# One layer of a sparse-attention, recurrence, cross-attention and product-key-expert block: recurrence gate moved to VectorE, attention units regrouped, cross attention by heads, expert decode in pieces

## The chip, the cores and the metric

One core of one Trainium2 chip (trn2) runs the whole kernel. The metric is the device time of one execution, in microseconds (us).

## The reference

The input `x` is 256 tokens by 1024 features (fp32). In order:

- `h = x @ w_in` gives the queries, keys, values and gates of everything below.
- **Sparse attention** (8 heads of 64, two key groups of four heads): per head a compressed branch (15 blocks of keys), a selected branch (with 4 blocks of 64 and 16 to be chosen, all are chosen, so it is causal attention over 256 keys with `k_slc, v_slc`) and a window branch (window 512, so causal attention with `k_win, v_win`). The branches are summed with sigmoid gates.
- **Recurrence** (4 heads of 128): `f = lb + (1 - lb) * sigmoid(...)`, a gated linear attention with decay `cumsum(log f)`; its output is normalised and multiplied by `norm_w` and by `silu(g)`.
- `x1 = LayerNorm(alpha * x + concat @ w_out)`.
- **Cross attention** over 256 memory tokens, 4 heads of 256: `softmax(q k^T / 16) v @ wo`, then `x2 = LayerNorm(alpha * x1 + ...)`.
- **Product-key experts**: per token and each of 8 heads, the top 16 of 128 + 128 half scores, the top 16 of their 256 sums, an expert number `i1 * 128 + i2` and a softmax gate for each; `a = gelu(down[e] . t) * gate`, `out = sum a * up[e]`, over 16384 experts. Then the last LayerNorm.

## The kernel before, in words

Every large matmul is done in three fp32r terms. A weight tile of 128x1024 fp32 (0.5 MB) is loaded by SyncE's queue into a slot `raw`; ScalarE rounds it to `hi` (`split`, L536); `lo = raw - hi` is made in the place of `raw` by VectorE (`rest`, L694) or by GpSimd (L522) for the tiles from `POOL_FROM` to `POOL_TO`; TensorE multiplies hi*hi, hi*lo and lo*hi (`three`, L1090 to L1092). There are `N1` = 75 stream tiles for all weights but the experts', then 128 `down` tiles and 128 `up` tiles. A tile of kind "T" is 24 matmuls of 256 columns, one of kind "R" 12 matmuls of 512 columns. ScalarE's `split` runs `DEPTH` = 4 tiles ahead. The `raw` ring has `EARLY` = 8 slots for the stream and `RING` = 5 for the experts; SyncE loads tile n once the tile that holds its slot was used. `slot(n)` gives the slot:

```python
return n % EARLY if n < N1 else (n - N1) % RING          # L182
POOL_FROM, POOL_TO = N1 - 4, N1 + 40                     # L179
```

`order()` writes the program order of the first part by hand, and every engine walks the same list in order; engines wait for each other by semaphores. In it the attention units `u` = 0 to 9 and the steps `level(j, t)` of the recurrence stand between weight tiles: per `u` a tile, `level(u-2, 0)`, the transposes of the probabilities of `u` (`turn_probs`), the scores of `u+1`, a tile, `level(u-2, 1)`, the values of `u`. After `level(j, 1)` VectorE merges (L936) and updates the factors `QF`, `KB` and `Fa`/`Fb` (L951 to L953), for which the next `level(j+1, 0)` (L1263) waits. Units 0 to 7 are a branch, a key group `g` and a half `t` of the tokens, four heads each: `scores` (L1140) makes for each head one or two 128-column blocks (L1171) with weights of 64 rows, each diagonal block followed by a matmul that adds the causal mask (L1174).

The gate `silu(g) * norm_w` is made by three GpSimd instructions (L504 to L508) when the `hg` tiles are done. Cross attention is units 10 and 11 (one half of the tokens each, four heads): both follow the eighth `xq` tile, and `turn` 4 and 5 (transposes of `xo`, L1309; rounding L651; rest L977) precede the first `xo` tile. Then come `xo`, the norm, eight `pq` tiles, each followed by `route(h)`: two score matmuls (L1285), and on VectorE the top-16 searches. When all eight are searched, VectorE decodes the positions to expert numbers (L992 to L1015: `picked_e` has 8192 f16 elements a partition), sums the gates (L1017 to L1021) and only then enters the loop over `down` and `up` tiles (`table_order()`), where `softmax` stands at tile 30 and `index` at tile 44. ScalarE writes gelu of each `down` tile (L660).

## Time and profile before

| | |
|---|---|
| median of 3 runs | 1169.48 us (1165.38 to 1171.67) |
| profiled execution, its own time | 1171.79 us |
| its span | 1170.0 us |
| mean granted TensorE clock | 0.971 |
| TensorE matmul / weight load busy | 94% / 85% |
| VectorE busy | 65% |
| ScalarE busy | 44% |
| GpSimd busy | 12% |
| moved from HBM | 183.80 MB, 158 GB/s |

The gelu of the first `down` tile starts at 391.4 us of the span, that of the last at 786.6 us; the `up` tiles take the rest. A group of matmuls that reads "busy" still overlaps its neighbours, so the distance from one start to the next is the time that one costs.

### The profile page before, as it was taken

The page shows a single profiled execution, that of the slowest core. Times are in us where ns is not written, and L with a number is a line of the kernel's source. Part 1 is how long each engine was busy: PE and PEld are TensorE (multiplying, and loading weights), DVE is VectorE, ACT ScalarE, POOL GpSimd, SP SyncE. Part 2 cuts the span into 40 slices and gives each one's busy share as a digit, 9 for nine tenths or more (in the row PEclk, how much of TensorE's full clock was granted, in tenths as well). Part 3 has the DMA queues.
Part 4 walks back from the last instruction along what each step waited for, and adds up shares of the span by engine and source line. Part 5 has one row for each costly group of instructions (what it writes and reads, how often), then busy time and mean ns, then how long its engine had stood idle before and what let it go on. Part 6 is the DMA issues. An engine that isn't in the chain of part 4 may idle for free.

```text
span 1170.0 us, 19066 instructions
## 1 busy us (share of the span) xinstructions
PE 1101.7 (94%) x7790; PEld 996.2 (85%) x7790; DVE 761.5 (65%) x1363; ACT 512.9 (44%) x799; POOL 146.1 (12%) x77
## 2 busy tenths in 40 slices
PE   6999989899869897999999999999999999999995
PEld 6987879779659897999999999998888788888884
DVE  4336555683377999124488888549888886555555
ACT  4244423444333443555544444454444444454451
POOL 3000020000004689930000000000000000000000
PEclk9889979999989999999999999999999999999998
DMA  9642212365031454555555445556555556556551
GB/s 335 220 154 91 80 65 83 114 203 198 28 117 38 163 182 126 179 181 180 180 163 163 163 162 164 179 183 206 172 176 168 178 166 190 186 195 193 188 195 73
DMA packets 50439, 186.62 MB, mean 160 GB/s; under 512 B 5824, under 2 KB 5856, under 8 KB 49840
## 3 DMA queue, kind: packets, MB, share of 16 engines
q1 hardware_dynamic: 48384, 176.71, 45.9%
q0 software_dynamic: 1968, 8.69, 2.2%
q8 instruction: 62, 1.02, 0.4%
q14 instruction: 25, 0.20, 0.1%
HBM read 183.80 MB, written 1.05 MB: 158 GB/s over the span
## 4 chain that ended last, share of the span: by engine, by line
PE 87%; DVE 5%; POOL 3%; ACT 2%; DMA 2%; issue 1%; SPq 0%; DVEq 0%; ACTq 0%
PE psS L1350 15%; PE psG L1090 15%; PE psT L1350 15%; PE psG L1091 14%; PE psG L1092 14%; POOL lo L522 3%; PE psS L1171 2%; PE psO L1334 1%; PE psO L1335 1%; PE psO L1263 1%; DMA raw<-in_down 1%; ACT hi L536 1%; PE psO L1231 1%; DVE lo L694 1%; PE psS L1163 1%
## 5 line engine op out<-in xcount | busy, mean ns | idle before, releaser
L694 DVE TENSOR_TENSOR lo<-raw,hi 128x1024 fp32r<-128x1024 f32 x287 | 350.0, 1221 | 220.2 <-ACT hi L536 219.9
L536 ACT ACTIVATE hi<-raw 128x1024 fp32r<-128x1024 f32 x331 | 350.3, 1059 | 308.1 <-DMA raw<-in_up 191.4
L1090 PE MATMUL psG<-b_hi,hi 128*128 128x256 f32 x1152 | 335.2, 291 | 9.1 <-POOL lo L522 7.5
L1091 PE MATMUL psG<-b_lo,hi 128*128 128x256 f32 x1152 | 329.3, 286 | 0.0
L1092 PE MATMUL psG<-b_hi,lo 128*128 128x256 f32 x1152 | 329.0, 286 | 0.0
L1090 PEld LDWEIGHTS psG<-b_hi,hi 128*128 128x128 f32 x1152 | 224.4, 195 | 11.1 <-POOL lo L522 8.9
L1091 PEld LDWEIGHTS psG<-b_lo,hi 128*128 128x128 f32 x1152 | 224.5, 195 | 0.2
L1092 PEld LDWEIGHTS psG<-b_hi,lo 128*128 128x128 f32 x1152 | 224.3, 195 | 0.0
L522 POOL TENSOR_TENSOR lo<-raw,hi 128x1024 fp32r<-128x1024 f32 x44 | 124.1, 2835 | 124.1 <-ACT hi L536 123.9
L1068 DVE TENSOR_TENSOR act_lo<-H,act_hi 128x256 fp32r<-128x256 f32 x128 | 54.0, 423 | 100.1 <-ACT act_hi L678 100.0
L660 ACT ACTIVATE H<-psG 128x256 f32<-128x256 f32 x128 | 49.1, 383 | 159.7 <-PE psG L1092 159.6
L1350 PE MATMUL psS<-hi,act_hi 128*128 128x512 f32 x256 | 82.3, 402 | 0.0
L1350 PE MATMUL psS<-hi,act_lo 128*128 128x512 f32 x256 | 79.5, 392 | 0.0
L1350 PE MATMUL psT<-hi,act_hi 128*128 128x512 f32 x256 | 79.5, 392 | 0.0
L1350 PE MATMUL psS<-lo,act_hi 128*128 128x512 f32 x256 | 79.4, 391 | 0.0
L1350 PE MATMUL psT<-lo,act_hi 128*128 128x512 f32 x256 | 79.3, 391 | 0.0
L1350 PE MATMUL psT<-hi,act_lo 128*128 128x512 f32 x256 | 79.2, 391 | 0.0
L1090 PE MATMUL psG<-o_hi,hi 128*128 128x256 f32 x192 | 59.2, 308 | 13.7 <-DVE lo L694 10.9
L1091 PE MATMUL psG<-o_lo,hi 128*128 128x256 f32 x192 | 58.0, 302 | 0.0
L1092 PE MATMUL psG<-o_hi,lo 128*128 128x256 f32 x192 | 57.9, 302 | 0.0
L1350 PEld LDWEIGHTS psT<-hi,act_hi 128*128 128x128 f32 x256 | 48.1, 188 | 10.7
L1350 PEld LDWEIGHTS psS<-lo,act_hi 128*128 128x128 f32 x256 | 48.1, 188 | 10.7
(273 smaller groups left out, 1523.3 us busy)
## 6 DMA issues: line engine op xcount, KB each, us to landing
raw<-in_down SPq DMA_DIRECT2D x128, 512.0 KB, 3.7
raw<-in_up SPq DMA_DIRECT2D x128, 512.0 KB, 3.9
raw<-in_w_stream SPq DMA_DIRECT2D x75, 512.0 KB, 3.8
w<-in_w POOLq DMA_DIRECT2D x1, 2048.0 KB, 8.6
xT<-in_xT SPq DMA_DIRECT2D x2, 512.0 KB, 4.7
memT<-in_memT SPq DMA_DIRECT2D x1, 1024.0 KB, 6.7
x_tok<-in_x_tok POOLq DMA_DIRECT2D x1, 1024.0 KB, 5.5
ln_gb<-in_ln_g POOLq DMA_DIRECT2D x2, 512.0 KB, 6.5
```

The lines of the kernel that those rows point to most:

```text
L522: pool.tensor_tensor(lo[slot(n)][:], raw[slot(n)][:], hi[n % DEPTH][:].bitcast(FP32), ALU.subtract)\
L536: act.activation(hi[n % DEPTH][:], raw[slot(n)][:], ACT.Copy).then_inc(hi_done, 1)
L660: act.activation(H[:, j, :], psG[j % 2][:, 0:S], ACT.Gelu).then_inc(h_out, 1)
L694: dve.tensor_tensor(lo[slot(n)][:], raw[slot(n)][:], hi[n % DEPTH][:].bitcast(FP32), ALU.subtract)\
L1068: dve.tensor_tensor(a_lo[j % 4][:], H[:, j, :], a_hi[j % 4][:].bitcast(FP32), ALU.subtract)\
L1090: pe.matmul(out, hi_l, hi_r, start=start, stop=False)
L1091: pe.matmul(out, hi_l, lo_r, start=False, stop=False)
L1092: return pe.matmul(out, lo_l, hi_r, start=False, stop=stop)
L1163: mm = pe.matmul(psS[:, h * S:(h + 1) * S], xq[:, 2 * h + kk, t * P:(t + 1) * P], xk[:, 2 * h + kk, :], start=kk == 0, stop=kk == 1)
L1171: mm = pe.matmul(out, qT[g * HD:(g + 1) * HD, r, t * P:(t + 1) * P], kT[b][g * HD:(g + 1) * HD, kb * P:(kb + 1) * P], start=True, stop=not ...
L1231: mm = pe.matmul(psM[:, kv * G * NC:(kv + 1) * G * NC], w1[:, kv, m, :], blk[:, kv, m, :], start=m == 0, stop=m == CB // 2 - 1)
L1350: mm = pe.matmul((psS, psT)[t][:, c * 512:(c + 1) * 512], left[:, cut], right[:, c * 512:(c + 1) * 512], start=st, stop=sp)
```

## The change

1. **Gate.** The three GpSimd instructions go. VectorE makes the gate in two steps `silu` (one for each half of the tokens, two instructions each), which stand behind the scores of units 7 and 8.
2. **Units.** A unit is now a branch, a pair `g` of head places and a half `t`: two heads of each key group. The mask goes first, one matmul for each of two PSUM banks over 256 or 512 columns, then one matmul for each head over all of its keys, heads of the two groups in turn. The number of exponentials, transposes and values is as before.
3. **Cross attention.** It is done by heads, both halves of the tokens together, in seven stages between the `xq` tiles (two a stage) and the first three `xo` tiles. An `xo` tile waits for its own head's part of `b_lo` alone.
4. **Ring.** The slots of the expert tiles are shifted by `N1 % EARLY` = 3.
5. **GpSimd's tiles** end at `N1 + 24` in place of `N1 + 40`.
6. **Decode.** It is cut into 8 steps at the `down` tiles 22, 24, ... 36, over half of the units of one list each, with layouts whose last dimension is a pair of f16 values; the gate sums follow the last step.

```diff
-UNITS = [(b, g, t) for b in range(2) for g in range(G) for t in range(NT)]
+UNITS = [(b, pair, t) for b in range(2) for pair in range(REP // 2) for t in range(NT)]
...
+        if u in (6, 7):
+            out.append(("silu", u - 6))
...
-    gemm(AT["xo"] - n)
-    out += [("scores", 10), ("turn_probs", 10), ("scores", 11), ("values", 10),
-            ("turn_probs", 11), ("values", 11), ("turn", 4), ("turn", 5)]
+    for stage in range(XH + 3):
+        gemm(2 if stage < XH else 1)
+        out += [(what, stage - lag) for lag, what in ((3, "cross_turn"), (2, "cross_values"), (1, "cross_probs"),
+                                                      (0, "cross_scores")) if 0 <= stage - lag < XH]
...
-POOL_FROM, POOL_TO = N1 - 4, N1 + 40
+POOL_FROM, POOL_TO = N1 - 4, N1 + 24
+DECODE = 8
...
-    return n % EARLY if n < N1 else (n - N1) % RING
+    return n % EARLY if n < N1 else (n - N1 + N1 % EARLY) % RING
...
+        if j >= 22 and j % 2 == 0 and (j - 22) // 2 < DECODE:
+            out.append(("decode", (j - 22) // 2))
...
-            pool.wait_ge(act_took, TAKEN[TILES[AT["hg"]][8] + 1][1])
-            pool.wait_ge(rec_in, 32)
-            pool.tensor_scalar(hg_t[:], hg_t[:], 1.0, 0.5, ALU.add, ALU.mult).then_inc(pool_step, 1)
-            pool.tensor_tensor(hg[:], hg[:], norm_w[:].unsqueeze(1).broadcast_to([P, NT, 512]), ALU.mult)\
-                .then_inc(pool_step, 1)
-            pool.wait_ge(pool_step, 2)
-            pool.tensor_tensor(hg[:], hg[:], hg_t[:], ALU.mult).then_inc(silu_ready, 1)
...
+                elif what == "silu":
+                    dve.wait_ge(act_took, TAKEN[TILES[AT["hg"]][8] + i][1])
+                    step(dve.scalar_tensor_tensor(out=hg[:, i, :], in0=hg_t[:, i, :], scalar=1.0, in1=hg[:, i, :],
+                                                  op0=ALU.add, op1=ALU.mult))
+                    step.wait()
+                    dve.scalar_tensor_tensor(out=hg[:, i, :], in0=hg[:, i, :], scalar=0.5, in1=norm_w[:],
+                                             op0=ALU.mult, op1=ALU.mult).then_inc(silu_ready, 1)
...
+            def decode(i):
+                c, first = i // 4, i // 2 % 2 * PH
+                units = slice(first, first + PH)
+                rows = PH * TOPK // 2
+                e = picked_e[:, c, units].rearrange("p u k a -> p (u k) a")
+                if i % 2 == 0:
+                    step(dve.tensor_tensor(e.rearrange("p n (a b) -> p n a b", b=2),
+                                           iota16[:].unsqueeze(1).broadcast_to([P, rows, TOPK, 2]),
...
+                                           .broadcast_to([P, rows, TOPK, 2]), ALU.is_equal))
+                    step.wait()
+                    step(dve.tensor_tensor(picked_e[:, c, units], picked_e[:, c, units],
...
+                for half in (16, 8, 4):
+                    step.wait()
+                    step(dve.tensor_tensor(e[:, :, 0:half], e[:, :, 0:half], e[:, :, half:2 * half], ALU.add))
...
+                if name == "xo" and i == 0:
+                    pe.wait_ge(cross_lo, k0 // 2 + 1)
...
-                for r in range(REP):
-                    for kb in range(t + 1):
-                        out = psS[:, r * S + kb * P:r * S + (kb + 1) * P]
-                        diagonal = kb == t
-                        mm = pe.matmul(out, qT[g * HD:(g + 1) * HD, r, t * P:(t + 1) * P],
-                                       kT[b][g * HD:(g + 1) * HD, kb * P:(kb + 1) * P], start=True, stop=not diagonal)
-                        if diagonal:
-                            mm = pe.matmul(out, identb[:], causal[:], start=False, stop=True)
+                for group in range(G):
+                    both = psS[:, group * 512:(group + 1) * 512].rearrange("p (j n) -> p j n", n=S)
+                    pe.matmul(both[:, :, 0:keys], identb[:],
+                              causal[:, S - keys:S].unsqueeze(1).broadcast_to([P, 2, keys]), start=True, stop=False)
+                for j in range(2):
+                    for group in range(G):
+                        at = (group * 2 + j) * S
+                        mm = pe.matmul(psS[:, at:at + keys], qT[group * HD:(group + 1) * HD, 2 * g + j, t * P:(t + 1) * P],
+                                       kT[b][group * HD:(group + 1) * HD, 0:keys], start=False, stop=j == 1)
...
+            def cross_scores(h):
+                pe.wait_ge(act_took, TAKEN[TILES[AT["xq"] + 2 * h + 1][8]][1])
+                if h >= 2:
+                    pe.wait_ge(cross_exp, h - 1)
```

On SyncE the loads stand at the change from the `pq` tiles (in_w_stream) to the `down` tiles as follows; `raw_58` to `raw_66` are slots 0 to 4, `raw_107` to `raw_111` slots 5 to 7. Before:

```order
L470 DMA raw_64<-in_w_stream 128x1024 [waits tile_used]
L470 DMA raw_66<-in_w_stream 128x1024 [waits tile_used]
L470 DMA raw_107<-in_w_stream 128x1024 [waits tile_used]
L470 DMA raw_109<-in_w_stream 128x1024 [waits tile_used]
L470 DMA raw_111<-in_w_stream 128x1024 [waits tile_used]
L470 DMA raw_58<-in_w_stream 128x1024 [waits tile_used]
L470 DMA raw_60<-in_w_stream 128x1024 [waits tile_used]
L470 DMA raw_62<-in_w_stream 128x1024 [waits tile_used]
L470 DMA raw_58<-in_down 128x1024 [waits tile_used]
L470 DMA raw_60<-in_down 128x1024 [waits tile_used]
L470 DMA raw_62<-in_down 128x1024 [waits tile_used]
```

Now, from the last three `pq` tiles on:

```order
L482 DMA raw_58<-in_w_stream 128x1024 [waits tile_used]
L482 DMA raw_60<-in_w_stream 128x1024 [waits tile_used]
L482 DMA raw_62<-in_w_stream 128x1024 [waits tile_used]
L482 DMA raw_64<-in_down 128x1024 [waits tile_used]
L482 DMA raw_66<-in_down 128x1024 [waits tile_used]
L482 DMA raw_58<-in_down 128x1024 [waits tile_used]
```

The first two `down` tiles now take the slots of the first two `pq` tiles, not of the sixth and seventh, and the third takes the slot of the sixth, not of the eighth.

On VectorE the cross attention stood in one piece before the `xo` tiles:

```order
L694 TENSOR_TENSOR lo_110<-raw_109,hi_56 128x1024
L751 TENSOR_REDUCE row_max<-psS 128x4
L754 TENSOR_SCALAR neg_max<-row_max 128x4
L751 TENSOR_REDUCE row_max<-psS 128x4
L754 TENSOR_SCALAR neg_max<-row_max 128x4
L768 RECIPROCAL coef<-row_sum 128x4
L783 TENSOR_TENSOR xo<-psO,coef 128x1024
L768 RECIPROCAL coef<-row_sum 128x4
L783 TENSOR_TENSOR xo<-psO,coef 128x1024
L977 TENSOR_TENSOR b_lo<-psS,b_hi 128x4x128 x2
```

Now its pieces stand between the weight tiles' `lo`; this is the fourth stage and the fifth:

```order
L726 TENSOR_TENSOR lo_108<-raw_107,hi_55 128x1024
L726 TENSOR_TENSOR lo_110<-raw_109,hi_56 128x1024
L978 TENSOR_TENSOR b_lo<-psT,b_hi 128x512
L798 RECIPROCAL coef<-row_sum 128x2
L802 TENSOR_TENSOR xo<-psO,coef 128x2x256
L790 TENSOR_REDUCE row_max<-psS 128x2
L793 TENSOR_SCALAR neg_max<-row_max 128x2
L726 TENSOR_TENSOR lo_112<-raw_111,hi_57 128x1024
L978 TENSOR_TENSOR b_lo<-psT,b_hi 128x512
```

The part of `b_lo` for a head stands behind the `lo` of the weight tiles of its stage.

On VectorE, behind the last search, the decode stood as one run:

```order
L998 CAST ranked_f<-ranked_i 128x512
L999 CAST picked_f<-picked_ab 128x512
L1001 TENSOR_TENSOR picked_e<-iota_87,picked_f 128x8192
L1008 TENSOR_TENSOR picked_e<-picked_e,ranked_f 128x4096 x2
L1013 TENSOR_TENSOR picked_e<-picked_e 128x512x8
L1013 TENSOR_TENSOR picked_e<-picked_e 128x512x4
L1013 TENSOR_TENSOR picked_e<-picked_e 128x512x2
L1015 TENSOR_TENSOR chosen<-picked_e 128x512
L1017 TENSOR_REDUCE gate_z<-chosen_s 128x16
```

Now it stands among VectorE's first `down` tiles (24 and on):

```order
L1060 CAST ranked_f<-ranked_i 128x1024
L1063 CAST picked_f<-picked_ab 128x512
L726 TENSOR_TENSOR lo_63<-raw_62,hi_57 128x1024
L726 TENSOR_TENSOR lo_65<-raw_64,hi_54 128x1024
L1072 TENSOR_TENSOR picked_e<-iota_87,picked_f 128x2048
L1078 TENSOR_TENSOR picked_e<-picked_e,ranked_f 128x2048
L726 TENSOR_TENSOR lo_67<-raw_66,hi_55 128x1024
L726 TENSOR_TENSOR lo_59<-raw_58,hi_56 128x1024
L1084 TENSOR_TENSOR picked_e<-picked_e 128x64x16
L1084 TENSOR_TENSOR picked_e<-picked_e 128x64x8
L1084 TENSOR_TENSOR picked_e<-picked_e 128x64x4
L1086 TENSOR_TENSOR chosen<-picked_e 128x128
```

One step of a quarter of the list now stands between every two `lo`.

## Rows read from the trace of the kernel before

**Rows 1.** The page, part 4: the chain that ended last, share by engine.

```profile
PE 87%; DVE 5%; POOL 3%; ACT 2%; DMA 2%; issue 1%; SPq 0%; DVEq 0%; ACTq 0%
```

**Rows 2.** 10-us stretches: length; PE, PEld, DVE, ACT, POOL busy; clock; DMA share; GB/s.

```profile
90.00:100.00 10.00, 8.71 (x60) 7.65 (x60) 5.88 (x13) 4.44 (x12) 0.00 (x0) 1.00 0.27 82
...
150.00:160.00 10.00, 5.44 (x22) 4.57 (x22) 7.29 (x9) 1.89 (x3) 3.59 (x2) 0.68 0.15 52
160.00:170.00 10.00, 10.00 (x56) 9.32 (x57) 2.21 (x3) 3.26 (x10) 0.00 (x0) 0.64 0.13 34
```

**Rows 3.** TensorE in order of time: start, us, line, tile, [idle before].

```profile
99.59 1.16 PE L1263 MATMUL psO<-hq,KB 128*128 128x128 f32 x8 [1.29 <-DVE QF L925]
...
144.21 1.06 PE L1263 MATMUL psO<-QF,KB 128*128 128x128 f32 x8
...
154.56 0.77 PE L1263 MATMUL psO<-QF,KB 128*128 128x128 f32 x2 [4.64 <-DVE Fb L953]
```

**Rows 4.** VectorE in order of time, two updates of the recurrence's factors.

```profile
135.48 0.67 DVE L951 TENSOR_TENSOR QF<-QF,Fb 128x512 f32<-128x512 f32 x1
...
149.23 2.24 DVE L951 TENSOR_TENSOR QF<-QF,Fa 128x512 f32<-128x512 f32 x1
151.39 2.82 DVE L952 TENSOR_TENSOR KB<-KB,Fa 128x512 f32<-128x512 f32 x1
```

**Rows 5.** GpSimd in order of time, the recurrence gate.

```profile
147.58 3.34 POOL L505 TENSOR_TENSOR hg<-hg,norm_w 128x1024 f32<-128x1024 f32 x1
```

**Rows 6.** TensorE in order of time, first row and follower of two score units.

```profile
126.03 0.71 PE L1171 MATMUL psS<-kT,qT 64*128 64x128 f32 x4
...
129.11 0.48 PE L1090 MATMUL psG<-hi,o_hi 128*128 128x512 f32 x1
...
139.17 0.49 PE L1171 MATMUL psS<-kT,qT 64*128 64x128 f32 x2
...
141.36 0.47 PE L1090 MATMUL psG<-hi,o_hi 128*128 128x512 f32 x1
```

**Rows 7.** The chain of waits, the cross attention: start, us, what.

```profile
288.33 3.71 PE psS L1163 x16
...
301.74 3.45 PE psO L1211 x16
...
313.83 0.47 PE psG L1090
```

**Rows 8.** The page, part 5: ScalarE's rounding and VectorE's rest of weight tiles.

```profile
L694 DVE TENSOR_TENSOR lo<-raw,hi 128x1024 fp32r<-128x1024 f32 x287 | 350.0, 1221 | 220.2 <-ACT hi L536 219.9
L536 ACT ACTIVATE hi<-raw 128x1024 fp32r<-128x1024 f32 x331 | 350.3, 1059 | 308.1 <-DMA raw<-in_up 191.4
```

**Rows 9.** TensorE and ScalarE in order of time, from the `pq` tiles to `down` 0.

```profile
355.34 1.03 PE L1285 MATMUL psO<-subk,qryT 128*128 128x256 f32 x4
...
359.08 1.03 PE L1285 MATMUL psS<-subk,qryT 128*128 128x256 f32 x4
...
374.18 1.06 ACT L536 ACTIVATE hi<-raw 128x1024 fp32r<-128x1024 f32 x1 [7.03 <-DMA raw<-in_down]
...
391.38 0.38 ACT L660 ACTIVATE H<-psG 128x256 f32<-128x256 f32 x1 [1.50 <-PE psG L1092]
394.26 0.38 ACT L660 ACTIVATE H<-psG 128x256 f32<-128x256 f32 x1 [1.55 <-PE psG L1092]
```

**Rows 10.** ScalarE, GpSimd and VectorE in order of time, the decode.

```profile
446.10 0.38 ACT L660 ACTIVATE H<-psG 128x256 f32<-128x256 f32 x1 [0.34 <-PE psG L1092]
...
479.82 0.38 ACT L660 ACTIVATE H<-psG 128x256 f32<-128x256 f32 x1 [1.35 <-PE psG L1092]
...
437.17 53.08 POOL L522 TENSOR_TENSOR lo<-raw,hi 128x1024 fp32r<-128x1024 f32 x15 [0.26 <-ACT hi L536]
...
437.57 10.78 DVE L1001 TENSOR_TENSOR picked_e<-iota,picked_f 128x8192 f16<-128x8192 f16 x1
```

**Rows 11.** Groups of instructions, VectorE: f16 pairs against a constant.

```profile
L1037 DVE TENSOR_TENSOR one<-iota,i2T 128x1024 f16<-128x1024 f16 x64 | 43.8, 685 | 0.0
```

More of the change, by code:

```diff
@@ L749, in max_unit @@
                     return
-                scale = HD ** -0.5 if b < 2 else (D // XH) ** -0.5
                 step(dve.tensor_reduce(row_max[:, 0:heads],
@@ L769, in combine @@
                 step.wait()
-                if b < 3:
-                    col = {0: 1, 1: 2, 2: 0}[b]
-                    gates = gate[:, t, :].rearrange("p (h c) -> p h c", c=3)[:, g * REP:g * REP + heads, col]
-                    step(dve.tensor_tensor(coef[:, 0:heads], coef[:, 0:heads], gates, ALU.mult))
-                    step.wait()
+                col = {0: 1, 1: 2, 2: 0}[b]
+                shape = [P, G, heads // G, HD]
+                first = g * 2 if b < 2 else 0
+                gates = gate[:, t, :].rearrange("p (g r c) -> p g r c", g=G, c=3)[:, :, first:first + heads // G, col]
+                by = coef[:, 0:heads].rearrange("p (g r) -> p g r", g=G)
+                step(dve.tensor_tensor(by, by, gates, ALU.mult))
+                step.wait()
                 if b == 2:
@@ L1005, in _ @@
-            step.wait()
-            for c in range(2):
-                e = picked_e[:, c].rearrange("p (u k) a -> p u k a", k=TOPK)
-                step(dve.tensor_tensor(e, e, ranked_f[:, :, c, :].unsqueeze(2).broadcast_to([P, PH * NT, TOPK, TOPK]),
-                                       ALU.mult))
-            e = picked_e[:].rearrange("p c n a -> p (c n) a")
-            for half in (8, 4, 2):
-                step.wait()
-                step(dve.tensor_tensor(e[:, :, 0:half], e[:, :, 0:half], e[:, :, half:2 * half], ALU.add))
@@ L1056, in _ @@
                     rest(UP + j + 3)
+                elif what == "decode":
+                    decode(j)
+                    if j == DECODE - 1:
+                        gate_weights()
                 elif what == "index":
@@ new lines, in cross_values @@
+            def cross_values(h):
+                pe.wait_ge(cross_probsT, h + 1)
+                if h >= 2:
+                    pe.wait_ge(cross_combined, h - 1)
+                width = D // XH
+                for t in range(NT):
+                    at = h % 2 * 512 + t * S
+                    for kb in range(2):
+                        mm = pe.matmul(psO[:, at:at + S], probsT[:, at + kb * P:at + (kb + 1) * P],
+                                       xv[:, kb, h * width:(h + 1) * width], start=kb == 0, stop=kb == 1)
+                mm.then_inc(cross_valued, 1)
```

211 lines of the change are left out of this document (139 added, 72 removed).

## The prediction

> **What bounds the kernel now.** I read the chain that ended last first: 87% of it is TensorE's [rows 1], so time is gained only where TensorE does less, waits less or runs at its full clock. Then I read TensorE in order of time, from start to start, for the places where a step costs more than its twin elsewhere. From the tile behind the decode on, a `down` tile costs 2.88 us (the distance between two gelus, [rows 9]) and the change leaves that work alone. What can move lies in five places ahead of about 480 us. In each the reader is to see one thing: which wait ends last there, and what the same step costs where nothing is late. The sum is made against the profiled execution's own 1171.8 us, which is 2.3 us above the median of the runs.
>
> **A. The gate (change 1).** `level(3, 1)` starts at 144.21, `level(4, 0)` at 154.56 with 4.64 us of idle before it [rows 3]. Ahead of it VectorE's two factor products took 2.24 and 2.82 us; the same form took 0.67 us one step earlier [rows 4]. Beside them ran GpSimd's gate instructions, the middle one 3.34 us long [rows 5]. Without them the products cost 0.67 each: 2.24 + 2.82 - 2 x 0.67 = 3.7 us gained, and 0.9 us of idle stays (VectorE first waits for ScalarE, which takes the `hg` tile in four pieces). In the trace the granted clock is 0.68 and 0.64 in the two stretches that hold this idle time and what follows [rows 2]; full clock is 2.4 GHz, the lower level 1.2. From 154.56 to the next `level` at 167.62 pass 13.1 us; the same steps cost at full clock 4.58 (level, transposes and a score unit, 3.08 of it the score unit of [rows 6], 0.97 a `level` and 0.53 four transposes in the same view) + 2.96 (the tile) = 7.5. So 5.5 us are the low clock. An idle time of 1.29 us before 99.59 [rows 3] stands in a stretch at clock 1.00 [rows 2], so I take it that 0.9 us will not lower the clock. A gives 3.7 + 5.5 = 9.2. Bounds: 1 (if the low clock stays and the two gate steps delay VectorE by their whole length) and 9.2. The added work is four VectorE instructions of 512 elements, some 0.7 us each by the products above, two behind the maximum of unit 7, two behind unit 8. I cost them at nothing: the weight tile's `lo` behind them can't begin before TensorE has ended the next tile (2.96 us) and ScalarE has rounded (1.06 us, [rows 8]), and the maximum (1.2) and the gate step (1.4) fit in. Without that cover it is 2.8 us.
>
> **B. Scores (change 2).** A unit with 256 keys cost 129.11 - 126.03 = 3.08 us, one with 128 keys 141.36 - 139.17 = 2.19 [rows 6]; there are four of each. Now each has two mask matmuls and four score matmuls (each fp32 one is two entries in the trace). The nearest entry of 256 fp32 columns is 3.71 / 16 = 0.23 us [rows 7]; for 128 columns I take half, 0.11. A mask over 512 columns I take at the 0.23 of 512 columns, though it is bf16. At each change between masks and scores I add 0.1, so 0.2 a unit. 256 keys: 2 x 0.23 + 8 x 0.23 + 0.2 = 2.5, 0.6 less. 128 keys: 2 x 0.12 + 8 x 0.11 + 0.2 = 1.3, 0.9 less. 4 x 1.5 = 5.8 us. TensorE is the engine that is late in these loops except just ahead of a factor update, whose own chain starts behind the score unit, so I count it all. Bounds: 0 (if each turn from one half of the rows to the other costs what a change costs now) and 11.3. The upper one is a rule of the Trainium skill, weighed in the rivals. The regrouped combine and the exponentials keep their counts and cost nothing.
>
> **C. Cross attention (change 3).** From the first score matmul to the first `xo` matmul pass 313.83 - 288.33 = 25.5 us [rows 7], and 0.5 us of waiting for the last `xq` copy lie ahead: 26.0. TensorE's work in it is two times scores of 3.7, values of 3.5 [rows 7], and transposes and turns of 0.9 each (8 entries of 128 columns at 0.11): 18. The other 8 are waits and some lower clock. After the change all this work stays, but stands between tiles, and its chains (maximum, exponentials, transposes, `b_hi`, `b_lo`) run beside tiles. Followed step by step, with 0.65 us for half of a VectorE or ScalarE instruction of [rows 8], these waits are left: 0.5 for the first `xq` copy; and, since ScalarE's rounding (1.06), VectorE's `lo` (1.22) and then `b_hi` and `b_lo` of the head come behind each `xo` tile, `b_lo` is ready 3.2 us after a tile's end. TensorE has 2.6, 2.2 and 0.45 us of other work there before the second, third and fourth `xo` tile: waits of 0.6, 1.0 and 2.7. With small gaps 5.1 in all, so C gives 8 - 5.1 = 2.9. Bounds 0 and 5. What is late next is `b_lo` of head 3.
>
> **D. Ring (change 4).** Two `pq` tiles with their route matmuls are 359.08 - 355.34 = 3.74 us apart [rows 9]. At that pace the last `pq` tile ends at 377.8, the last two routes at 379.7 and gelu 0 would start at 382.6. It starts at 391.38 [rows 9]: 8.8 us late. The reason stands at 374.18: ScalarE waited 7.03 us for the load of `down` 0 [rows 9], which had to wait for the sixth `pq` tile, and ScalarE's copies of `pq` results stand behind it. Now the first two loads go four and more tiles earlier, and the third has one tile's lead, as in the steady part, where TensorE doesn't wait. D gives 8.8; bounds 6 and 8.8. Nothing else is late there: the searches (VectorE) hold nobody.
>
> **E. Decode (changes 5, 6).** From gelu at 446.10 to that at 479.82 are 8 tiles [rows 10], 33.7 us in place of 8 x 2.88 = 23.0: 10.7 us lost. GpSimd makes every `lo` there, 53.08 / 15 = 3.5 us each [rows 10], slower than the 2.88 of a tile, beside VectorE's long f16 instructions, the first of 10.78 us [rows 10]. Now GpSimd stops at `down` 23, and VectorE does the decode in quarters among its own `lo`. Price of the pieces: pairs of f16 against a constant cost 0.69 us for 1024 elements [rows 11], so 2048 cost 1.3; with a product of 2048 and sums of 1024 and less a quarter costs 4.3, 17 in all, 1.1 a tile. With `lo` (1.22) VectorE is busy 2.3 of each 2.88 us. Hidden; E gives 10.7, bounds 4 and 10.7. The handover: the searches and casts end at 437.57, where the first long instruction starts [rows 10], on a chain of VectorE's own that D doesn't move. TensorE, earlier by D, wants `down` 24 at 379.7 + 24 x 2.88 = 448.8, so its `lo` has to begin by 447: 9 us to spare.
>
> **Sum.** 9.2 + 5.8 + 2.9 + 8.8 + 10.7 = 37.4 us. 1171.8 - 37.4 = 1134.4; against the median 1132.1. I predict 1133.
>
> **The rivals.**
> 1. *The two row halves run together.* In each unit two heads have weights and keys in partitions 0 to 63, two in 64 to 127, and the changed order takes them in turn, into different banks. If a score matmul of one half runs beside one of the other, 8 entries cost as much as 4: 4 x (0.92 + 0.44) = 5.5 us more, 1128. For it: only half of the array's rows is used by such a matmul. Against: the trace before has no two neighbours of this kind, and every entry of [rows 7] follows the one before it. The Trainium skill, "TensorE: Matmul & The Clock Gate", Part 3, states that matmuls on different row groups run concurrently; no row of this trace shows it. The sum by that rule is the one just given.
> 2. *The clock still falls in the recurrence.* The idle time shrinks to 0.9 us, but the stretch between 150 and 170 us has many short matmuls. Then 5.5 us are not gained: 1139. Against: the row at 99.59.
> 3. *VectorE becomes the bound in the decode.* If the pieces cost what the run did before (about 34 us) the 16 tiles need 34 + 16 x 1.22 = 53.5 us of VectorE and have 46. Late by 7.4, less about 1 of lead: 1140. It decides from 3.8 us for a piece on. Against: 0.69 us for 1024 pairs [rows 11].
> 4. *The handover comes too early, and the kernel is slower.* `down` 24 waits for VectorE's searches. Each us that these end later than the 9 us to spare is lost. To be 6 us slower than now they would have to end 9 + 37 + 6 = 52 us later, the search 127 us long in place of 75. The nearest reason is GpSimd's `lo` beside them, which stretched two-input products by 3 to 4 times [rows 4], but it already stands beside them now.
>
> **How the numbers follow.** Forecast 0.45 (1133, its own range 1128 to 1138), rival 1 0.25 (1128), rival 2 0.12 (1139), rival 3 0.12 (1140), several terms at their lower bounds at once 0.04 (1145 to 1165), rival 4 0.02. The range 1122 to 1146 leaves out the last two and the far edges. Half a percent, 5.8 us, is about what a measurement of this kernel tells from no change: faster 0.96, same 0.02, slower 0.02.
>
> **What would show it.** A: factor products at 0.67 everywhere and clock 1.00 where 0.68 and 0.64 stood. B: score units of 2.5 and 1.3 us; 1.6 and 0.9 if rival 1 holds. C: from the start of the `xq` tiles to the end of the fourth `xo` tile 3 us less, with the longest wait at `b_lo` of head 3. D: ScalarE's waits for `in_down` of 1 us, gelu 0 3.7 us after the last route begins. E: gelus 2.88 us apart from 0 to 40, GpSimd's `lo` at 2.4 us. I would be wrong if gelus spread between tiles 22 and 38, or if TensorE waits at a place that is now covered.

## The result, and the profile after

| | before | after |
|---|---|---|
| median | 1170.58 us (1165.38 to 1176.26, 4 runs) | 1127.26 us (1121.88 to 1128.02, 4 runs) |
| profiled execution, its own time | 1171.79 | 1128.02 |
| its span | 1170.0 | 1125.8 |
| mean granted TensorE clock | 0.971 | 0.980 |

The ratio is 0.9619, 95% interval 0.9565 to 0.9674: faster, by 43.3 us of medians and by 44.2 us of span. The forecast was 1133 with a range of 1122 to 1146. Rival 1, the two row halves side by side, gave 1128.

The page of the changed kernel, its part 1 (busy time, share, instructions) and part 4 (the chain that ended last, by engine), against [rows 1]:

```profile
PE 1077.1 (96%) x7742; PEld 977.2 (87%) x7742; DVE 767.1 (68%) x1408; ACT 512.4 (46%) x801; POOL 83.9 (7%) x58
...
PE 88%; DVE 6%; ACT 3%; issue 1%; DMA 1%; SPq 0%; DVEq 0%; ACTq 0%
```

GpSimd has left the chain (it held 3%). TensorE is busy for 96% of the span; before it was 94%.

**Where the 44.2 us went**, from the start-to-start distances of both traces:

| place | before | after | gained | forecast |
|---|---|---|---|---|
| A. `level(3,1)` to `level(4,0)` | 10.35 | 6.63 | 3.7 | 3.7 |
| A. `level(4,0)` to `level(4,1)`, without B's share of 1.5 | 13.06 | 5.97 | 5.6 | 5.5 |
| B. score unit, 256 keys, four of them | 3.08 | 1.59 | 4 x 1.49 = 6.0 | 2.3 |
| B. score unit, 128 keys, four of them | 2.19 | 0.96 | 4 x 1.23 = 4.9 | 3.5 |
| C. first `xq` tile to the second half of the last `xo` tile | 61.69 | 58.86 | 2.8 | 2.9 |
| D. first route matmul to the first gelu | 36.04 | 27.24 | 8.8 | 8.8 |
| E. first gelu to the gelu of `down` 50 | 155.34 | 145.26 | 10.1 | 10.7 |
| sum | | | 41.9 | 37.4 |

The 2.3 us that are missing to 44.2 lie ahead of the recurrence (1.6, low clock) and behind `down` 50 (1.0), less 0.3 between. A part of what the table gains is TensorE's clock and not its work: the trace before has stretches at the lower of the two levels behind some of its long waits, and these are gone with the waits. A, C and D below say how much that is. All runs together show it too. The lower level is half of full clock, so 2 x (1 - mean granted clock) x span is the time spent there: as an estimate 71 us in the mean of the 11 runs of the kernel before beside `after_again` (clock 0.9696) and 41 us in the 5 runs of the changed kernel (0.9818). Half of the difference, at most 15 of the 43 us, is what the clock gave.

**A.** TensorE of the changed kernel in order of time, from `level(4,0)` to `level(4,1)`; left out are the unit's score entries and one weight tile. [rows 3] has the wait of 4.64 us that stood there:

```profile
139.93 1.13 PE L1379 MATMUL psO<-QF,KB 128*128 128x128 f32 x8 [0.92 <-DVE Fb L1015]
140.90 0.60 PE L1261 MATMUL psT<-ident,probs 128*128 128x128 f32 x4
141.34 0.59 PE L1239 MATMUL psS<-causal,identb 128*128 128x512 bf16 x2
...
145.90 0.83 PE L1379 MATMUL psO<-QF,KB 128*128 128x128 f32 x6
```

VectorE there: the two factor products, against 2.24 and 2.82 us in [rows 4], and behind unit 7 the new gate step with what follows it:

```profile
138.31 0.68 DVE L1013 TENSOR_TENSOR QF<-QF,Fa 128x512 f32<-128x512 f32 x1
138.90 0.68 DVE L1014 TENSOR_TENSOR KB<-KB,Fa 128x512 f32<-128x512 f32 x1
139.50 0.28 DVE L1015 TENSOR_TENSOR Fb<-Fa 128x128 f32<-128x128 f32 x1
...
144.38 0.68 DVE L963 SCALAR_TENSOR_TENSOR hg<-hg_t,hg 128x512 f32<-128x512 f32 x1
145.09 0.69 DVE L966 SCALAR_TENSOR_TENSOR hg<-hg,norm_w 128x512 f32<-128x512 f32 x1
147.69 1.23 DVE L726 TENSOR_TENSOR lo<-raw,hi 128x1024 fp32r<-128x1024 f32 x1 [1.90 <-ACT hi L540]
```

The products are back at 0.68. Behind the gate step VectorE still waits 1.90 us for ScalarE, so the moved work costs almost nothing: from `level(4,1)` to `level(5,0)` pass 5.12 us here and 4.92 in `u1_gate_on_gpsimd`, which is the same kernel without it. The stretches (columns as in [rows 2]) that hold the wait and what follows it:

```profile
130.00:140.00 10.00, 9.08 (x69) 8.27 (x67) 4.76 (x10) 6.16 (x16) 0.00 (x0) 1.00 0.19 57
140.00:150.00 10.00, 10.00 (x82) 9.19 (x83) 7.69 (x12) 4.12 (x12) 0.00 (x0) 1.00 0.34 105
```

Full clock in both, where 0.68 and 0.64 stood.

**B.** A score unit with 256 keys on TensorE, against 3.08 us in [rows 6]:

```profile
118.02 0.59 PE L1239 MATMUL psS<-causal,identb 128*128 128x512 bf16 x2
118.55 1.13 PE L1244 MATMUL psS<-kT,qT 64*128 64x256 f32 x8
119.61 0.50 PE L1168 MATMUL psG<-hi,o_hi 128*128 128x512 f32 x1
```

From 118.02 to 119.61 pass 1.59 us, 1.06 of them for eight score entries. The same trace, instruction by instruction, has their starts at 118.547 and 118.554, 118.867 and .874, 119.083 and .089, 119.299 and .305: pairs 6 to 7 ns apart, 216 ns from pair to pair. Eight entries take the time of four.

**C.** TensorE before the second, third and fourth `xo` tile:

```profile
285.54 0.47 PE L1168 MATMUL psG<-hi,b_hi 128*128 128x512 f32 x1 [0.55 <-DVE b_lo L978]
...
291.67 0.47 PE L1168 MATMUL psG<-hi,b_hi 128*128 128x512 f32 x1 [0.99 <-DVE b_lo L978]
...
297.80 0.47 PE L1168 MATMUL psG<-hi,b_hi 128*128 128x512 f32 x1 [2.72 <-DVE b_lo L978]
```

The forecast had 0.6, 1.0 and 2.7, each on `b_lo`. Gone are the waits of 3.48 us for `probs` and 1.11 us for `probsT`, which the kernel before has on TensorE:

```profile
295.51 1.09 PE L1192 MATMUL psT<-ident,probs 128*128 128x128 f32 x8 [3.48 <-ACT probs L581]
296.44 5.30 PE L1163 MATMUL psS<-xk,xq 128*128 128x256 f32 x16
...
307.43 3.72 PE L1211 MATMUL psO<-xv,probsT 128*128 128x256 f32 x16 [1.11 <-ACT probsT L595]
```

The middle line is low clock behind the first wait: the same 16 entries took 3.71 us in [rows 7]. So about 1.4 of the 2.8 us that C gained are clock. `b2_mask_first_one_half`, which has the old cross attention, has low clock only at the first `xq` tile, as the changed kernel has, and needs 60.23 us for the stretch of the table, 1.4 more than the changed kernel.

**D.** ScalarE around the first `down` tiles, where [rows 9] has 7.03 us of waiting for `in_down`:

```profile
354.28 1.06 ACT L540 ACTIVATE hi<-raw 128x1024 fp32r<-128x1024 f32 x1 [0.17 <-DMA raw<-in_down]
...
358.33 0.38 ACT L692 ACTIVATE H<-psG 128x256 f32<-128x256 f32 x1 [0.37 <-PE psG L1170]
...
361.21 0.39 ACT L692 ACTIVATE H<-psG 128x256 f32<-128x256 f32 x1 [1.55 <-PE psG L1170]
```

The first two gelus are 2.88 us apart; nothing is late at the handover. What was late before is seen on TensorE of that kernel in order of time, and in the stretch that holds it (columns as in [rows 2]):

```profile
385.87 2.07 PE L1285 MATMUL psS<-subk,qryT 128*128 128x256 f32 x4 [4.89 <-ACT qryT L553]
```

```profile
380.00:390.00 10.00, 5.11 (x24) 4.28 (x24) 10.00 (x57) 5.51 (x11) 6.12 (x3) 0.83 0.45 157
```

With another wait of 1.91 us at 376.11 TensorE waits 6.8 us here; the other 2.0 of the 8.8 are low clock behind the wait. All four traces with the old ring have a low-clock stretch in this place (before, b1, b2, u3: 36.04, 35.91, 38.93 and 35.95 us from the first route matmul to the first gelu), and the ten with the new one have none (27.24 in each).

**E.** VectorE from the end of the searches through the first quarter of the decode:

```profile
415.91 2.63 DVE L1063 CAST picked_f<-picked_ab 128x512 f16<-128x512 uint32 x1
418.66 1.23 DVE L726 TENSOR_TENSOR lo<-raw,hi 128x1024 fp32r<-128x1024 f32 x1
...
422.49 1.22 DVE L1072 TENSOR_TENSOR picked_e<-iota,picked_f 128x2048 f16<-128x2048 f16 x1
423.75 1.23 DVE L1078 TENSOR_TENSOR picked_e<-picked_e,ranked_f 128x2048 f16<-128x2048 f16 x1
...
428.11 1.47 DVE L1084 TENSOR_TENSOR picked_e<-picked_e 128x1024 f16<-128x1024 f16 x3
429.61 0.29 DVE L1086 TENSOR_TENSOR chosen<-picked_e 128x128 f32<-128x128 f16 x1
```

A quarter costs 1.22 + 1.23 + 1.47 + 0.29 = 4.2 us (forecast 4.3), against 10.78 us for the first instruction alone in [rows 10]. The first `lo` on VectorE, for `down` 24, starts at 418.66; gelu 24 could start at 358.33 + 24 x 2.88 = 427.5, its tile 3 us before. That `lo` had to begin by 423.0, so some 4 us are to spare; the forecast had 9. The chain from the first route matmul to the last cast has become 5 us longer (331.09 to 418.5; before 355.34 to 437.57). In it waits for GpSimd have moved about among short instructions: `picked_f` took 2.63 us for 0.41 before, the `chosen_s` product 2.51 for 0.43, `ranked_f` 0.68 for 2.63, and 2.6 us more lie elsewhere in the searches. The gelus of `down` 0 to 30 are 2.88 us apart without an exception.

### The profile page after: what moved, and what is told of

Read it like the earlier page. It is cut to its first block, busy times and chain, and to the rows that moved or that the text cites. A ratio compares the mean times of both kernels' runs of the same rounds, so it can differ in the third digit from the quotient of the medians.

```text
span 1125.8 us, 19010 instructions
## 1 busy us (share of the span) xinstructions
PE 1077.1 (96%) x7742; PEld 977.2 (87%) x7742; DVE 767.1 (68%) x1408; ACT 512.4 (46%) x801; POOL 83.9 (7%) x58
## 4 chain that ended last, share of the span: by engine, by line
PE 88%; DVE 6%; ACT 3%; issue 1%; DMA 1%; SPq 0%; DVEq 0%; ACTq 0%
PE psS L1462 16%; PE psG L1168 16%; PE psT L1462 15%; PE psG L1170 15%; PE psG L1169 15%; PE psO L1446 1%; PE psO L1447 1%; ACT hi L540 1%; DVE lo L726 1%; PE psO L1379 1%; PE psO L1339 1%; DVE x L762 1%; PE psS L1293 1%; DMA raw<-in_w_stream 1%; ACT probs L584 1%
## 5 line engine op out<-in xcount | busy, mean ns | idle before, releaser
L726 DVE TENSOR_TENSOR lo<-raw,hi 128x1024 fp32r<-128x1024 f32 x303 | 369.5, 1221 | 218.0 <-ACT hi L540 217.5
L1168 PE MATMUL psG<-b_hi,hi 128*128 128x256 f32 x1152 | 331.8, 288 | 1.9 <-DVE b_lo L1039 1.5
L1168 PEld LDWEIGHTS psG<-b_hi,hi 128*128 128x128 f32 x1152 | 221.8, 193 | 3.0 <-issue 2.8
L1169 PEld LDWEIGHTS psG<-b_lo,hi 128*128 128x128 f32 x1152 | 221.9, 193 | 0.2
L1170 PEld LDWEIGHTS psG<-b_hi,lo 128*128 128x128 f32 x1152 | 221.7, 192 | 0.0
L526 POOL TENSOR_TENSOR lo<-raw,hi 128x1024 fp32r<-128x1024 f32 x28 | 69.0, 2464 | 111.7 <-ACT hi L540 111.6
L1462 PEld LDWEIGHTS psT<-hi,act_lo 128*128 128x128 f32 x256 | 48.1, 188 | 10.5
L1462 PEld LDWEIGHTS psT<-lo,act_hi 128*128 128x128 f32 x256 | 48.1, 188 | 10.4
```

The source lines that it names most:

```text
L526: pool.tensor_tensor(lo[slot(n)][:], raw[slot(n)][:], hi[n % DEPTH][:].bitcast(FP32), ALU.subtract)\
L726: dve.tensor_tensor(lo[slot(n)][:], raw[slot(n)][:], hi[n % DEPTH][:].bitcast(FP32), ALU.subtract)\
L1168: pe.matmul(out, hi_l, hi_r, start=start, stop=False)
L1169: pe.matmul(out, hi_l, lo_r, start=False, stop=False)
L1170: return pe.matmul(out, lo_l, hi_r, start=False, stop=stop)
L1462: mm = pe.matmul((psS, psT)[t][:, c * 512:(c + 1) * 512], left[:, cut], right[:, c * 512:(c + 1) * 512], start=st, stop=sp)
```

## The experiments

Ten edits ran, and two kernels twice (`after_again` is the changed kernel, `v1_again` is `v1_b_first` once more), each beside runs of the kernel before on the same chip.

| label | median us | ratio to before | 95% interval |
|---|---|---|---|
| after_again | 1127.50 | 0.9625 | 0.9602 to 0.9648 |
| u1_gate_on_gpsimd | 1132.02 | 0.9664 | 0.9627 to 0.9701 |
| b1_before_gate_on_vector | 1165.94 | 0.9962 | 0.9942 to 0.9983 |
| u2_halves_in_turn_off | 1128.64 | 0.9639 | 0.9602 to 0.9676 |
| b2_mask_first_one_half | 1164.04 | 0.9941 | 0.9918 to 0.9965 |
| u3_ring_back | 1132.52 | 0.9677 | 0.9634 to 0.9721 |
| u4_gpsimd_to_40 | 1124.58 | 0.9599 | 0.9560 to 0.9637 |
| u5_decode_in_one | 1139.18 | 0.9743 | 0.9695 to 0.9790 |
| u6_decode_in_one_gpsimd_40 | 1127.79 | 0.9635 | 0.9593 to 0.9677 |
| v1_b_first | 1121.00 | 0.9596 | 0.9547 to 0.9644 |
| v1_again | 1123.05 | 0.9592 | 0.9568 to 0.9616 |
| v2_hg_split_first | 1121.05 | 0.9588 | 0.9564 to 0.9612 |

> The changed kernel once more, as the measure for the three others: 1124 to 1128 us, 0.962 of the kernel before, within the interval of the first measurement.

It measured 1127.50 (1125.04 to 1128.44), ratio 0.9625.

### A: the gate

`u1_gate_on_gpsimd`: the changed kernel with the three GpSimd instructions back and without the two `silu` steps.

```diff
-        if u in (6, 7):
-            out.append(("silu", u - 6))
...
+            pool.tensor_scalar(hg_t[:], hg_t[:], 1.0, 0.5, ALU.add, ALU.mult).then_inc(pool_step, 1)
+            pool.tensor_tensor(hg[:], hg[:], norm_w[:].unsqueeze(1).broadcast_to([P, NT, 512]), ALU.mult)\
+                .then_inc(pool_step, 1)
...
+            pool.tensor_tensor(hg[:], hg[:], hg_t[:], ALU.mult).then_inc(silu_ready, 1)
```

> The changed kernel (1127.3 us) with the gate back on GpSimd. Theory (GpSimd's two-input instructions stretch VectorE's factor products): the pair of products beside GpSimd takes 4.5 to 5 us again in place of 1.4, TensorE's wait before the fifth level step grows from 0.9 to about 4.6 us. If that wait is also what lowers the clock, 5.5 us of low clock follow: 1127.3 + 3.7 + 5.5 = 1136.5. Rival (the low clock there has another cause, such as the run): only the wait comes back, 1131, and the clock stays at 1.00 behind it.

1132.02 us. Its VectorE in order of time:

```profile
135.64 2.23 DVE L1019 TENSOR_TENSOR QF<-QF,Fa 128x512 f32<-128x512 f32 x1
137.79 2.82 DVE L1020 TENSOR_TENSOR KB<-KB,Fa 128x512 f32<-128x512 f32 x1
```

Its GpSimd:

```profile
133.99 3.33 POOL L515 TENSOR_TENSOR hg<-hg,norm_w 128x1024 f32<-128x1024 f32 x1
```

And its TensorE:

```profile
140.96 2.05 PE L1385 MATMUL psO<-QF,KB 128*128 128x128 f32 x8 [4.64 <-DVE Fb L1021]
142.80 1.06 PE L1267 MATMUL psT<-ident,probs 128*128 128x128 f32 x4
143.66 1.06 PE L1245 MATMUL psS<-causal,identb 128*128 128x512 bf16 x2
144.65 2.08 PE L1250 MATMUL psS<-kT,qT 64*128 64x256 f32 x8
...
149.84 1.05 PE L1385 MATMUL psO<-QF,KB 128*128 128x128 f32 x8
```

With GpSimd's instructions the 2.24, 2.82 and 4.64 us of the kernel before are back to within 0.01. Behind the wait each step lasts about twice as long (0.99 for the masks and 2.01 for the scores from start to start, 0.52 and 1.06 in the changed kernel); the granted clock of 140 to 150 us is 0.66, with the lower of the two levels, 1.2 GHz, in its first part. From 140.96 to the next level are 8.88 us, 5.97 in the changed kernel: 2.9 us of low clock here, 5.6 in the kernel before.

`b1_before_gate_on_vector`: the same part alone, put into the kernel before (the diff of u1 the other way round).

> The kernel before (1170.6 us) with the gate on VectorE, and nothing else. Theory: the products take 0.7 us each, the wait of 4.64 us becomes 0.9. With the clock as in the prediction -9.2: 1161.4. Rival (no part of the low clock belongs to that wait): -3.7, 1166.9.

1165.94 (10 runs) against 1168.57 (13 runs): 2.6 us less by the medians, 4.4 by the ratio (2.0 to 6.8 by its interval). That holds the rival's 3.7 and leaves out the theory's 9.2. In its trace the wait and the low clock behind it are gone: from `level(3,1)` to `level(4,1)` are 6.63 + 7.53 = 14.2 us in place of 10.35 + 13.06 = 23.4, so 9.2 us are gained there. Its profiled execution took 1162.12, the fastest of its ten; over all runs the gain is half of that or less. The 3.7 us of wait are in each trace. Of the 5.5 us of clock the runs show little: b1 gained 2.6 or 4.4, u1 lost 4.5 us of medians against after_again (4.6 by the ratios, with intervals too wide to leave out 9.2). The clock of all runs says the same: the mean granted clock is 0.9707 over the 13 runs before and 0.9716 over the 10 of b1, where the two profiled executions have 0.971 and 0.976. By the estimate used above that is 2.4 us less at the lower level, worth 1.2 us. Which stretches run at the lower level differs between executions (b1 has 0.83 at 100 to 110 us and 0.74 at 280 to 290, where the trace of before has full clock), and only profiled executions tell where.

### B: the scores

`u2_halves_in_turn_off`: the changed kernel with both heads of one group first, then both of the other.

```diff
-                for j in range(2):
-                    for group in range(G):
+                for group in range(G):
+                    for j in range(2):
```

> The changed kernel with the two heads of one key group behind each other, then those of the other: the same matmuls, the same masks. Theory (matmuls on the two row halves run in pairs only where they are neighbours): a score part of 256 keys goes from 1.06 to 1.7 to 1.85 us, of 128 keys from 0.65 to 0.9, +1131 to 1132 us in all. One pair may be left in the middle. Rival (the gain is from longer matmuls and fewer changes between masks and scores): both stay, 1127.

1128.64 us, and the same 1.59 and 0.96 us. The score entries again start in pairs, 13 ns apart (118.927 and .941, 119.247 and .261, and so on). The order in the program doesn't matter here. The trace doesn't say which rows an entry uses, but entries of one half start 216 ns apart (in `b2_mask_first_one_half` below), so I read each pair as one of either half. As each matmul is two entries, the first entry of the second half then starts ahead of three entries of the first half that stand before it in the program. The forecast of 1131 to 1132 failed, and this edit didn't tell the theories apart by time; `b2_mask_first_one_half` had to. It is the kernel before with the masks first and matmuls of 256 columns, but with units of one key group, so that no two score matmuls use different rows:

```diff
-                    for kb in range(t + 1):
-                        out = psS[:, r * S + kb * P:r * S + (kb + 1) * P]
-                        diagonal = kb == t
...
+                    mm = pe.matmul(psS[:, r * S:r * S + keys], qT[g * HD:(g + 1) * HD, r, t * P:(t + 1) * P],
+                                   kT[b][g * HD:(g + 1) * HD, 0:keys], start=False, stop=r % 2 == 1)
```

> The kernel before, with one part of the change: each bank's masks go first, as one matmul of 512 columns, and the scores of two heads follow as one matmul of 256 columns; but a unit is still four heads of one key group, so that all its scores use one half of TensorE's rows. Theory (the merging gives what the prediction's sum said, and the rest comes from the two row halves side by side): a unit's masks and scores last 2.5 us at 256 keys and 1.3 us at 128 keys, start to start, against 3.08 and 2.19 before and 1.59 and 0.96 in the changed kernel; over eight units of each kind about 5.8 us less than before, near 1164 us if before is near 1170. Rival (the merging alone gives all of it): 1.6 and 0.96 us, and near 1159 us.

1164.04 us against 1170.20. Its TensorE, the unit that answers to the one shown for the changed kernel:

```profile
117.94 0.59 PE L1169 MATMUL psS<-causal,identb 128*128 128x512 bf16 x2
118.47 1.99 PE L1172 MATMUL psS<-kT,qT 64*128 64x256 f32 x8
120.39 0.50 PE L1090 MATMUL psG<-hi,o_hi 128*128 128x512 f32 x1
```

2.45 us, and 1.40 with 128 keys: the 2.5 and 1.3 of the forecast. The eight entries start one by one, 216 ns apart (320 behind the first). Masks cost the same 0.53 in both kernels; only the score entries halve, 1.92 to 1.06. That is the two halves of the rows side by side, and nothing else of the change. It gives 4 x (0.86 + 0.44) = 5.2 us more. By the Trainium skill, "TensorE: Matmul & The Clock Gate", Part 3, matmuls on different row groups run concurrently; the trace agrees (6 to 13 ns from start to start). The same part says that matmuls start in program order; for u2's order the trace differs, if the pairs are read as above.

The trace of the kernel before did hold such neighbours, in a place that the forecast had not looked at. Its TensorE, the scores of the compressed branch (15 columns; heads 0 to 3 in the first rows, then heads 4 to 7):

```profile
174.45 1.53 PE L1151 MATMUL psS<-kcmp,qT 64*128 64x15 f32 x16
175.91 0.39 PE L1090 MATMUL psG<-b_hi,hi 128*128 128x256 f32 x1
```

Sixteen entries in 1.46 us; the first ones start 0.112 apart, and 16 x 0.112 would be 1.8. Instruction by instruction, starts at 174.916 and 174.922, then 175.029 and 175.055, show the two groups overlapping in time.

### D: the ring

`u3_ring_back`:

```diff
-    return n % EARLY if n < N1 else (n - N1 + N1 % EARLY) % RING
+    return n % EARLY if n < N1 else (n - N1) % RING
```

> The changed kernel with the slots of the expert tiles as before. Theory: ScalarE waits about 7 us for the load of down 0 again, and the first gelu starts 35.9 us after the first route's matmuls in place of 27.2: 1127.3 + 8.7 = 1136. Rival (part of it is hidden now by GpSimd's or VectorE's place in the order): 2 to 5 us.

1132.52 us. Its ScalarE at the handover:

```profile
346.95 1.06 ACT L540 ACTIVATE hi<-raw 128x1024 fp32r<-128x1024 f32 x1 [6.92 <-DMA raw<-in_down]
...
364.17 0.38 ACT L692 ACTIVATE H<-psG 128x256 f32<-128x256 f32 x1 [1.43 <-PE psG L1170]
```

The wait of [rows 9] is back (6.92 for 7.03), and from the first route matmul to the first gelu are 35.95 us: 8.7 more than 27.24, of which 6.7 are TensorE's waits (1.79 and 4.90) and 2.0 low clock. The medians show 5.0 more than after_again, the ratios 0.0052, 6 us: between the rival's 5 and the theory's 8.7. The wait is shown in the trace; why the medians show less is not. Its profiled execution had reached the first route matmul 2.9 us sooner than the changed kernel's, because the stretches at 180 and at 240 us had full clock in it and 0.83 in the other.

### E: the decode

Three edits take the parts of the change apart. `u4_gpsimd_to_40` lets GpSimd make the `lo` of `down` up to 39 again (`N1 + 40`). `u5_decode_in_one` makes all eight decode steps ahead of the loop, still with the short pair instructions. `u6_decode_in_one_gpsimd_40` does both, so that of the change only the new layouts and the quarters remain.

```diff
-        if j >= 22 and j % 2 == 0 and (j - 22) // 2 < DECODE:
-            out.append(("decode", (j - 22) // 2))
...
+            for i in range(DECODE):
+                decode(i)
+                step.wait()
```

> The changed kernel, but GpSimd keeps the lo of the first 40 down tiles; the decode stands in pieces in the same places. Theory (a two-input instruction of one of the two engines waits for the other's): with 4.2 us of decode for every four tiles GpSimd's tile goes from 2.4 to about 3.4 us, over 2.88, and TensorE loses some 0.5 us a tile over 16 tiles less 3.4 us of lead: +5, 1132. Rival (pieces this short fit into GpSimd's gaps): 1127 to 1128.

> The changed kernel (GpSimd to down 23, pair layouts), but the eight decode steps follow each other ahead of VectorE's loop. Theory: 17 us of steps from 418.6 to 435.5 stand ahead of the lo of down 24, which TensorE wants at 424.2: it waits 11 to 13 us, 1139. Rival (VectorE's share of the lo could start late without harm): 1127 to 1130.

> The same one run of eight short-layout steps, with GpSimd's lo to down 39 as in the kernel before: the layouts alone. Theory (each of GpSimd's lo waits for one VectorE instruction, now 1.2 us and not 10.8): GpSimd's tile costs 2.4 + 1.2 = 3.6 us for the 17 to 25 us of the run, 5 to 7 tiles, 0.7 us late each, less 3.4 us of lead: +0 to 2, 1127 to 1129. Rival (the loss goes by busy time): half of the 10.7 us lost before, 1132.

1124.58, 1139.18 and 1127.79 us. u4's theory (+5) failed, u5's and u6's held. u5: ScalarE's gelus at the end of GpSimd's tiles:

```profile
419.06 0.38 ACT L690 ACTIVATE H<-psG 128x256 f32<-128x256 f32 x1 [0.42 <-PE psG L1173]
437.67 0.38 ACT L690 ACTIVATE H<-psG 128x256 f32<-128x256 f32 x1 [15.99 <-PE psG L1173]
```

Two gelus 18.6 us apart, 15.7 too many: `down` 24 waits for its `lo` behind 17 us of decode. TensorE's wait is 13.12 us, just above the 11 to 13 that were forecast; the rest is low clock (0.61 granted from 430 to 440 us). With GpSimd stopping at 23, the spreading is needed. u6, in one run again but with GpSimd to 39, loses nothing. Its VectorE:

```profile
419.40 3.32 DVE L1076 TENSOR_TENSOR picked_e<-picked_e,ranked_f 128x2048 f16<-128x2048 f16 x1
```

Its GpSimd:

```profile
418.45 16.76 POOL L524 TENSOR_TENSOR lo<-raw,hi 128x1024 fp32r<-128x1024 f32 x6 [0.62 <-ACT hi L538]
435.55 14.15 POOL L524 TENSOR_TENSOR lo<-raw,hi 128x1024 fp32r<-128x1024 f32 x5 [0.35 <-ACT hi L538]
```

Here VectorE's instructions are the ones that suffer: 3.32 us in place of 1.23. GpSimd makes a `lo` in 16.76 / 6 = 2.79 us, under the 2.88 of a tile. In the kernel before it took 3.5 in the mean [rows 10]: one of 10.64 beside the f16 instruction of 10.78, and three of 4.42 beside those of 4.3 to 4.5. Each engine waits for the other's whole instruction, so a short instruction harms GpSimd little. It is the length of one instruction that counts, and not VectorE's time beside GpSimd: the decode of u6 is 24 instructions that last 50 us in all, against 7 with 34 us in the kernel before, and GpSimd still keeps up. The Trainium skill, "SBUF — State Buffer", "two separate sides", calls the pair of ports that these two engines share an exclusive lock held for the whole instruction; the trace agrees (1.23 + most of a 2.4-us `lo` makes 3.32).

So E's 10 us come from the short f16 instructions, alone and whole. GpSimd's earlier end and the spreading are two edits that cancel: u6 has neither and stands at 0.9635, within the interval of after_again. u4 is the same as u6 where it runs: with no `lo` of its own between the steps, VectorE makes them one behind the other, from 418.17 to 469.0 us in u4 and from 418.14 to 469.1 in u6. Its GpSimd:

```profile
421.15 16.29 POOL L526 TENSOR_TENSOR lo<-raw,hi 128x1024 fp32r<-128x1024 f32 x6 [0.61 <-ACT hi L540]
```

That is 2.7 us for a `lo`, where u4's forecast had 3.4. From the first gelu to that of `down` 50 u4 takes 145.88 us, u6 145.53 and the changed kernel 145.26: u4's lower median (ratio 0.9599, not separated by the intervals) is no gain of the decode.

### C: what was late next

`v1_b_first` goes after the three waits of C: ScalarE's rounding and VectorE's `lo` of the next weight tile, which stand behind each of the first three `xo` tiles, move behind the head's `b_hi` and `b_lo`.

```diff
+BEHIND_TURN = [AT["xo"] + i for i in range(3)]
...
-                    split(i + DEPTH)
+                    if i not in BEHIND_TURN:
+                        split(i + DEPTH)
...
+                    if i:
+                        rest(BEHIND_TURN[i - 1] + DEPTH)
```

> The changed kernel; in the three stages with an xo tile ScalarE's and VectorE's part of the head's b goes ahead of the rounding and the lo of the weight tile. Theory (b_lo behind the tile's hi and lo is what TensorE waits for): the steps before the second, third and fourth xo tile (1.15, 2.89 and 3.32 us now) go to 0.45, 1.75 and 1.8: 3.4 us less, 1124. Rival (the waits are the chain through the exponentials and the values): nothing changes.

> The same kernel as v1_b_first, beside the changed kernel on one chip: the move of VectorE's work ahead of the xo tiles takes 3.3 us of idle time of TensorE in the traces, so the time is 3 to 4.7 us under after_again. If the earlier difference (6 us of medians) was the chip's spread, it is less than 2 us here.

1121.00 and 1123.05 us, the second 4.5 us under after_again on its chip (3.9 by the ratios). C's stretch of the table takes 54.2 us in `v1_again`, against 57.44 in the two traces of the old order that have full clock there (u3, u5): 3.2 us less. Of the waits of 0.55, 0.99 and 2.72 us TensorE has one left (`v1_again`):

```profile
289.22 0.47 PE L1174 MATMUL psG<-hi,b_hi 128*128 128x512 f32 x1 [1.50 <-DVE b_lo L982]
```

`v2_hg_split_first` adds to v1 one more such swap, for the 0.92 us before `level(4,0)`: ScalarE rounds the next tile first and then takes the last bank of `hg`.

```diff
+                    if i == AT["mk"] - 1:
+                        split(i + DEPTH)
```

> The kernel of v1_b_first, and ahead of the first matmul of level 4, ScalarE rounds the next weight tile only after it has taken the last bank of hg. Theory: TensorE's wait of 0.92 us before level 4 is the time of that rounding, so it goes, and the time is 0.9 us under v1_again. Rival: the wait is the chain of VectorE's operations themselves, or the weight tile comes late in its place; no difference from v1_again.

In its trace the wait is gone; `level(3,1)` to `level(4,0)` are 5.55 us in place of 6.63; the step to `level(5,0)` gives 0.3 of that back (5.42 for 5.12). Its median of 1121.05 is 2.0 us below v1_again, but the means of the runs, 1122.2 and 1122.4, are alike: 0.9 us is under what these runs resolve. v1 and v2 beat both kernels: the mean of after_again is 1127.2, of v1's ten runs on two chips 1122.1.

## Why the prediction came out as it did

- **The total** was 5.7 us too high, within the range. One step failed (B, 5.1 us too small) and one term has an uncertain size (A). That the total fits rival 1's 1128 so well is in part luck: 2.3 us lie outside the five places and go with the clock, and A's 5.5 us are not in the medians as a step of their own.
- **A.** The trace gained 3.7 + 5.6, as the sum had it, and the gate step is hidden but for 0.2 us. Rival 2, low clock in spite of the shorter wait, did not come: no trace of a kernel with the gate on VectorE has a lower clock between 130 and 160 us, and all three with it on GpSimd (before, u1, b2) have one. But 5.5 us came from one execution. In u1 the same wait brought 2.9, and b1 and u1 hold 2.6 and 4.5 us of medians for all of A (4.4 and 4.6 by the ratios). The mechanism stands; the 5.5 us were the size of one trace, not of the median. An idle time of 0.9 us did not lower the clock, as row 99.59 had promised.
- **B** was the step that failed: "Against: the trace before has no two neighbours of this kind". It has them, at L1151, and they overlap. The 5.8 us for merging alone were right (b2: 6.2 us of medians; 5.7 us from its durations). The other 5.2 us are rival 1, which had 5.5 us and a chance of 0.25. Had the search for such neighbours gone by tiles with 64-row weights, not by the units alone, the forecast would have been 1128.
- **C** came out to a tenth in the sum and in each wait. The 8 us of "waits and some lower clock" held 1.4 us of clock from one execution, though; b2's trace, without it, puts C at 1.4 us. `b_lo` of head 3 was the longest, and v1 shows that most of these waits were the order of ScalarE's and VectorE's own work.
- **D** is exact in the traces (8.8 forecast, 8.8 and 8.7 measured by the change and by its undoing). The text named only the wait as its reason: that is 6.8, and 2.0 are the clock behind it, which came in as the distance was read from the trace.
- **E** gave 10.1 for 10.7. Rival 3 did not come: the two pieces of a quarter took 4.2 us together, 2.1 each, and it needed 3.8 for one. Rival 4 still had 4 us to go before it cost anything, not 9, since the chain of searches grew by 5 us where the forecast took it as unmoved. What the text did not see is that the short instructions alone do it. It argued with VectorE's load among its own `lo`, and that is needed only because GpSimd stops at 23.

**What stays open.** The 2.3 us outside the five places go with the clock, and no run isolates them. Why the clock behind the same wait costs 2.9 us once and 5.6 us another time is not shown. The eight merged `row_max` and exponentials were not tried apart, and neither were the pair layout and the cut into quarters.

## What to carry to other kernels

Search the trace for any pair of neighbours that already does what the change wants (here weights in different halves of the rows), even at 15 columns: it answers a question that argument can't. If two engines get in each other's way by whole instructions, shorten the long ones before moving work between the engines. And where a term is read as a distance in one trace, take the wait and the low clock behind it apart: the wait comes back in each execution, and the clock may be counted as possible, not as the median's.
